# Chunk chain with its products grouped by kind and the next level's operand made early, and row transposes spread over the attention rounds

## The reference, cut to what matters

```python
zs = z[..., :SHIFT_COLS]                                   # 1792 columns
zs_mix = zs + w['mu_shift'] * (prev - zs)                  # prev: the row before
# RWKV-7 recurrence, a state of 64 x 64 per head, 8 heads
def step(s, inp):
    r_t, d_t, k_t, v_t, kk_t, a_t = inp
    sa = jnp.einsum('bhij,bhj->bhi', s, kk_t)
    s = (s * d_t[:, :, None, :] - sa[..., None] * (kk_t * a_t)[:, :, None, :]
         + v_t[..., None] * k_t[:, :, None, :])
    return s, jnp.einsum('bhij,bhj->bhi', s, r_t)
# forgetting attention of the prompt, 128 queries at a time
s = jnp.einsum('bqhd,bkhd->bhqk', q_i, k) * scale + F_i - Fk     # causal
p = jax.nn.softmax(s, axis=-1)
# attention of the samples over 4096 cached tokens: softmax(...) @ past_v
return y, k, v, logf, wkv_new, zs[:, -1]                   # also outputs
```

## Time and profile before

| what | us |
|---|---|
| median of 3 runs | 2940.16 (2926.0 to 2944.49) |
| the profiled execution: its own time | 2937.45 |
| its span on the core | 2935.7 |
| from the end of `z13` to the first scores of FOX (308.4 to 337.6) | 29.2 |
| FOX (337.6 to 600) | 262.4 |
| CHAIN (743 to 1160) | 417.0 |
| of which the four stretches of levels | 61.1, 64.3, 62.8, 63.0 |
| and the four stretches of two chunks | 31.9, 30.7, 30.3, 29.0 |
| QUERY's end and PEER (1510 to the end) | 1425.7 |

### The profile page before, as it was taken

One profiled execution on the slowest core, in us unless ns is written; L12 is line 12 of the kernel. 1 busy time (PEld: TensorE's weight loads), 2 busy tenths in 40 slices (PEclk: granted clock), 3 DMA queues, 4 the chain that ended last, 5 costly groups with the idle time before them and its releaser, 6 DMA issues.

```text
span 2935.7 us, 29533 instructions
## 1 busy us (share of the span) xinstructions
PE 2215.7 (75%) x9678; PEld 881.1 (30%) x9678; DVE 1666.6 (57%) x3582; ACT 240.9 (8%) x476; POOL 1353.8 (46%) x1559
## 2 busy tenths in 40 slices
PE   5999699942799898685892057777677777777998
PEld 3345355531454454342551011111111111111222
DVE  2588477547321221515279976676666667666812
ACT  1111211121010111100100000000000000000000
POOL 0233122100223332000058877777777777777755
PEclk7999789966878988897896589999999999999989
DMA  7377455435445545131079899999999999999988
GB/s 257 126 255 233 154 191 180 144 102 190 136 138 186 159 154 195 40 135 57 33 277 329 287 371 409 407 405 385 379 399 408 408 379 392 401 408 406 404 322 315
DMA packets 238555, 774.79 MB, mean 264 GB/s; under 512 B 32360, under 2 KB 34124, under 8 KB 237912
## 3 DMA queue, kind: packets, MB, share of 16 engines
q0 software_dynamic: 191008, 680.63, 62.7%
q1 hardware_dynamic: 47424, 92.54, 9.0%
HBM read 763.01 MB, written 10.04 MB: 263 GB/s over the span
## 4 chain that ended last, share of the span: by engine, by line
PE 39%; POOL 25%; DVE 14%; issue 12%; DMA 4%; POOLq 3%; ACT 1%; SPq 1%; PEldq 0%; DVEq 0%; ACTq 0%; PEld 0%
POOL arena L739 25%; PE bank L764 18%; DVE arena L2056 5%; PE bank L1186 5%; PE bank L907 3%; POOLq L717 2%; PE bank L903 2%; PE bank L1027 2%; DMA arena<-in_peer_v,arena 2%; PE bank L770 1%; SPq L563 1%; PE bank L1220 1%; PE bank L894 1%; PE bank L895 1%; PE bank L1084 1%
## 5 line engine op out<-in xcount | busy, mean ns | idle before, releaser
L1186 PE MATMUL bank<-arena 128*32 128x512 f32 x2048 | 889.6, 607 | 280.0 <-DMA arena<-in_peer_v,arena 275.8
L2056 DVE CUSTOM_DVE_ANT_0 arena<-arena 128x1024 f32<-128x1024 f32 x512 | 623.5, 1223 | 329.6 <-DMA arena<-in_peer_u,arena 328.0
L739 POOL DMA_INDIRECT arena<-in_peer_u,arena x520 | 566.2, 1089 | 501.8 <-DVE arena L1927 319.0
L764 PE MATMUL bank<-arena 128*128 128x8 f32 (+5 forms) x2088 | 589.8, 433 | 44.8 <-DVE arena L1772 23.9
L739 POOL DMA_INDIRECT arena<-in_peer_v,arena x520 | 509.8, 980 | 193.0 <-issue 141.6
L1186 PEld LDWEIGHTS bank<-arena 128*32 128x32 f32 x2048 | 180.2, 110 | 984.2 <-DMA arena<-in_peer_v,arena 654.3
L764 PEld LDWEIGHTS bank<-arena 128*128 128x128 f32 (+3 forms) x2088 | 309.4, 185 | 320.8 <-issue 282.9
L722 POOL DMA_DIRECT2D arena<-in_cache_v x256 | 137.7, 538 | 449.8 <-PE bank L1027 274.3
L722 POOL DMA_DIRECT2D arena<-in_cache_k x256 | 137.8, 538 | 414.1 <-issue 223.3
L770 PE MATMUL bank<-arena 128*128 128x128 f32 (+5 forms) x350 | 64.8, 323 | 244.2 <-DVE arena L1927 79.5
L1554 DVE TENSOR_TENSOR arena<-arena 128x512 f32<-128x512 f32 x256 | 175.4, 685 | 68.9 <-ACT arena L1242 51.0
(11 more groups left out here) (252 smaller groups left out, 1524.7 us busy)
## 6 DMA issues: line engine op xcount, KB each, us to landing
arena<-in_cache_k POOLq DMA_DIRECT2D x256, 256.0 KB, 3.5
arena<-in_cache_v POOLq DMA_DIRECT2D x256, 256.0 KB, 3.4
arena<-in_w_ada SPq DMA_DIRECT2D x12, 2048.0 KB, 10.5
arena<-in_w_in SPq DMA_DIRECT2D x10, 2048.0 KB, 10.3
arena<-in_peer_u,arena POOLq DMA_INDIRECT x520, 6.6
arena<-in_peer_v,arena POOLq DMA_INDIRECT x520, 6.6
arena<-in_peer_wq SPq DMA_DIRECT2D x4, 2048.0 KB, 7.9
arena<-scratch_gates SPq DMA_DIRECT2D x16, 260.0 KB, 2.7
```

Source lines behind the costliest of these rows:

```text
L739: nc.gpsimd.indirect_dma_start(gathered[:, j, :], None, tables[kind[0]][:, :], OFF(ap=index, axis=0)).then_inc(row_in[j], 16)
L764: ins = mm(out, a, b, start=i == 0, stop=i == len(pairs) - 1, **more)
L1186: ins = mm(acc[u][32 * j:32 * (j + 1), :], spread[:, token(x), :], gathered_row(("v", t, x))[:, 512 * u:512 * (u + 1)], start=x < 4, stop= ...
L2056: release(nc.vector.tensor_tensor_reduce(out=row, in0=row, in1=h2[:, t, :], scale=1.0, scalar=0.0, op0=MUL, op1=ADD, accum_out=act_of[t % ...
```

## The change

Three things are changed in PROJ and FOX. The eight row jobs (`shift0` to `shift3`, `krows0` to `krows3`) leave the end of PROJ; they are made in rounds 1, 5, 9, ..., 29 of FOX, their stores follow the gate stores on SP's queue, and the next writer of their buffer waits for the store's own semaphore. The exponential and logarithm of the forget logits are taken by ACT behind `z10`, and DVE's sum along the tokens behind its addition for block 11. The one addition of 7280 columns becomes 14 of 512 columns, each behind a share of the cached key pages, and one small one for the samples.

Two things are changed in CHAIN. DVE makes the next level's `xt` as soon as `iy` has been read, ahead of the two subtractions; PE waits for `inv` ahead of `iy` and for `inv_t` ahead of `inv`. In `r` and `oc` two matmuls with a buffer of zeros first open the whole sum (64 partitions, 256 columns each, one for each half of the partitions), then come the eight products over 64 partitions, then the eight over 128.

```diff
+ROWS_OUT = {4 * u + 1: f"shift{u}" for u in range(4)}
+ROWS_OUT.update({4 * t + 17: f"krows{t}" for t in range(NT)})
...
@@ sync @@
-            for u in range(4):
-                read(sp, f"shift{u}")
...
-                sp.wait_ge(stored, OUTPUTS[0])
-                sp.sem_inc(shift_stored, 1)
...
             for m in range(16):
                 read(sp, f"gc{m}")
                 load(scratch_g[:, m, 0:T], gate_rows[:, m % 2, :], gates_out[m % 2])
+                if m % 2 == 0 and m < 8:
+                    u = m // 2
+                    read(sp, f"shift{u}")
...
+                if m % 2 == 0 and m >= 8:
+                    t = m // 2 - 4
+                    read(sp, f"krows{t}")
+                    load(nk[:, t, :], buf("k_rows"), krows_out)
@@ tensor, FOX @@
+                if i in ROWS_OUT:
+                    job = ROWS_OUT[i]
+                    o = begin(job)
+                    if i < 16:
+                        for k in range(min(4, MS - (i - 1))):
+                            ins = turn(o[0:9, P * k:P * (k + 1)], z9[:, i - 1 + k, :])
+                    else:
+                        t = (i - 17) // 4
+                        for c in range(NC):
+                            ins = turn(o[:, P * c:P * (c + 1)], k_t[:, c, P * t:P * (t + 1)])
+                    end(ins, job)
@@ tensor, CHAIN @@
+                def open_sums(o):
+                    for a in (0, C):
+                        mm(o[a:a + C, 0:NC * C], ident[a:a + C, a:a + C], buf("zeros")[a:a + C, :], start=True, stop=False)
                 for lv in range(LEVELS):
                     pe.wait_ge(xt_ready, 2 * (gp * LEVELS + lv + 1))
+                    if lv:
+                        read(pe, f"inv{gp}_{lv - 1}")
                     small(f"iy{gp}_{lv}", xt, inv)
                     page_values(gp, 3 * lv, points)
                     read(pe, f"iy{gp}_{lv}")
+                    if lv:
+                        read(pe, f"invt{gp}_{lv - 1}")
...
                     o = begin(f"r{n}")
+                    open_sums(o)
                     for h, c, a in heads:
-                        mm(o[a:a + C, C * c:C * (c + 1)], rk[a:a + C, c, n, 0:C], state[a:a + C, c, :],
-                           start=True, stop=False)
-                        ins = mm(o[a:a + C, C * c:C * (c + 1)], g[:, e2, h, 0:C], uv[:, s, h, :], start=False, stop=True)
+                        mm(o[a:a + C, C * c:C * (c + 1)], rk[a:a + C, c, n, 0:C], state[a:a + C, c, :], start=False, stop=False)
+                    for h, c, a in heads:
+                        ins = mm(o[a:a + C, C * c:C * (c + 1)], g[:, e2, h, 0:C], uv[:, s, h, :], start=False, stop=c == NC - 1)
@@ scalar, PROJ @@
+                if m == 10:
+                    act.wait_ge(f_abs, 1)
+                    link(fn(f2[0:8, 0:TT], f2[0:8, 0:TT], ACT.Exp))
+                    link(fn(f2[0:8, 0:TT], f2[0:8, 0:TT], ACT.Ln, bias=1.0), signal=f_log, at=1)
@@ vector, PROJ @@
-            page_dots(96, 136)
...
-            link(tt(buf("mix"), buf("mix"), buf("prev"), ADD))
+            for m in range(MS):
+                page_dots(96 + 40 * m // MS, 96 + 40 * (m + 1) // MS)
+                read(dve, f"z{m}")
+                link(tt(mix[:, m, 0:T], mix[:, m, 0:T], prev[:, m, 0:T], ADD))
...
@@ vector, CHAIN @@
-                for lv in range(LEVELS):
-                    if lv:
-                        full(dve, f"iy{gp}_{lv - 1}")
+                def level(lv):
...
+                level(0)
+                for lv in range(LEVELS):
+                    if lv + 1 < LEVELS:
+                        full(dve, f"iy{gp}_{lv}")
+                        level(lv + 1)
```

More of the change, by code:

```diff
@@ L136 @@
     ("wring0", 4096, LOAD, QUERY), ("wring1", 4096, LOAD, QUERY),
-    ("mix", MS * TT, PROJ, MIX), ("prev", MS * TT, PROJ, PROJ), ("z9", MS * 9, PROJ, PROJ),
+    ("mix", MS * TT, PROJ, MIX), ("prev", MS * TT, PROJ, PROJ), ("z9", MS * 9, PROJ, FOX),
     ("shift_out", 512, PROJ, SAMPLE),
@@ L188, in psum_jobs @@
     fixed(7, "zs")
-    ring(*[f"shift{u}" for u in range(4)], *[f"krows{t}" for t in range(NT)], "logf")
+    ring("logf")
     fixed(7, "gs")
@@ L196, in psum_jobs @@
             ring(f"gc{i // 2}")
+        if i in ROWS_OUT:
+            ring(ROWS_OUT[i])
         if 2 <= i < NT * H + 2:
@@ L868, in _ @@
             read(pe, "zs")
-            for u in range(4):
-                o = begin(f"shift{u}")
-                for i in range(min(4, MS - 4 * u)):
-                    ins = turn(o[0:9, P * i:P * (i + 1)], z9[:, 4 * u + i, :])
-                end(ins, f"shift{u}")
-            for t in range(NT):
-                o = begin(f"krows{t}")
-                for c in range(NC):
-                    ins = turn(o[:, P * c:P * (c + 1)], k_t[:, c, P * t:P * (t + 1)])
-                end(ins, f"krows{t}")
             pe.wait_ge(logf_ready, 1)
@@ L1095, in _ @@
                     o = begin(f"oc{n}")
+                    open_sums(o)
                     for h, c, a in heads:
-                        mm(o[a:a + C, C * c:C * (c + 1)], state[a:a + C, c, :], rk[a:a + C, c, n, C:P],
-                           start=True, stop=False)
-                        ins = mm(o[a:a + C, C * c:C * (c + 1)], uv[:, s, h, :], g[:, e2, h, C:P], start=False, stop=True)
+                        mm(o[a:a + C, C * c:C * (c + 1)], state[a:a + C, c, :], rk[a:a + C, c, n, C:P], start=False, stop=False)
+                    for h, c, a in heads:
+                        ins = mm(o[a:a + C, C * c:C * (c + 1)], uv[:, s, h, :], g[:, e2, h, C:P], start=False, stop=c == NC - 1)
                     end(ins, f"oc{n}")
@@ L1287, in _ @@
                 take(f"z{m}", z9[:, m, 8:9], o[:, T - 1:T])
+                if m == 10:
+                    act.wait_ge(f_abs, 1)
+                    link(fn(f2[0:8, 0:TT], f2[0:8, 0:TT], ACT.Exp))
+                    link(fn(f2[0:8, 0:TT], f2[0:8, 0:TT], ACT.Ln, bias=1.0), signal=f_log, at=1)
             take("zs", z9[:, :, 0:8], bank("zs")[:, 0:MS * NS].rearrange("p (m b) -> p m b", m=MS))
-            for u in range(4):
-                n = min(4, MS - 4 * u) * P
-                if u:
-                    act.wait_ge(shift_stored, u)
-                take(f"shift{u}", buf("shift_out")[0:9, 0:n], bank(f"shift{u}")[0:9, 0:n])
-            for t in range(NT):
-                if t:
-                    act.wait_ge(krows_out, t)
-                take(f"krows{t}", buf("k_rows"), bank(f"krows{t}")[:, :])
-            act.wait_ge(f_abs, 1)
-            link(fn(f2[0:8, 0:TT], f2[0:8, 0:TT], ACT.Exp))
-            link(fn(f2[0:8, 0:TT], f2[0:8, 0:TT], ACT.Ln, bias=1.0), signal=f_log, at=1)
             take("logf", buf("logf_out"), bank("logf")[:, 0:NT * H])
@@ L1322, in _ @@
                     take(f"gc{m}", gate_rows[:, m % 2, :], bank(f"gc{m}")[:, :])
+                if i in ROWS_OUT and i < 16:
+                    u = i // 4
+                    n = min(4, MS - 4 * u) * P
+                    if u:
+                        act.wait_ge(shift_stored, 32 * u)
+                    take(f"shift{u}", buf("shift_out")[0:9, 0:n], bank(f"shift{u}")[0:9, 0:n])
+                if i in ROWS_OUT and i >= 16:
+                    t = (i - 17) // 4
+                    if t:
+                        act.wait_ge(krows_out, 16 * t)
+                    take(f"krows{t}", buf("k_rows"), bank(f"krows{t}")[:, :])
                 if i >= 3 and (i - 3) % H == H - 1:
@@ L1328, in _ @@
             act.wait_ge(gates_out[1], 8 * 16)
+            act.wait_ge(shift_stored, 4 * 32)
+            act.wait_ge(krows_out, NT * 16)
             act.wait_ge(proj_stored, 1)
@@ L1717, in _ @@
                 link(nc.vector.memset(removed[a:a + C, :, :, a // C, :], 0.0))
+            link(nc.vector.memset(buf("zeros"), 0.0))
             link(nc.vector.memset(buf("state"), 0.0), signal=state_ready, at=1)
```

31 lines of the change are left out of this document (17 added, 14 removed).

## The result

| | before | changed |
|---|---|---|
| median of 4 runs | 2937.51 (2926.0 to 2944.49) | 2901.78 (2892.78 to 2917.92) |
| profiled execution: its own time | 2937.45 | 2901.79 |
| its span | 2935.7 | 2900.1 |

The ratio of the times is 0.9872, with a 95% interval of 0.9838 to 0.9907. The gain is 36 us: inside the range, and smaller than the 54 of the forecast.

The account below looks back on a forecast made before the run. Bounds: a chain of waits before FOX, PE in FOX and CHAIN's chunks, POOL's page issuing in the levels. Terms -25.8 + 5 - 1 - 32 = -53.8 gave 2886.4, stated as 2885, range 2867 to 2903.

Parts of the forecast that it names:

- The stretch before FOX: End of PROJ: FOX starts at 311.8 instead of 337.64, -25.8 us, with bounds of -24.8 and -26.1.
- Forecast +4: FOX: +5 us for 30 added transposes (bounds 4 and 8.1), together with -1 for the clock.
- The -1 for a clock that rises sooner: FOX's first rounds: a shorter gap before them removes some low-clock time, -1 us, between 0 and -2.
- Forecast -32: CHAIN's chunks: shorter sums save 36.6 us, late pages take some back; bounds -24 to -37.
- The term that was mis-sized: CHAIN, `r` and `oc`: each sum takes 0.70 + 0.58 + 0.68 = 1.96 us instead of 4.54 and 3.96.
- a rival at 12%: CHAIN's chunks: the clock stays up without the alternation, perhaps 2 us a group more, 2877 in all; 12%.
- the 1.2 us a group of the forecast: CHAIN's chunks: time put down for pages that arrive late once the sums are shorter, 1.2 us a group.
- Halves of the array in one bank: CHAIN's sums: the halves do not overlap in a shared bank, a sum takes 2.98 us, 2898 in all; 10%.
- The early `xt`: CHAIN's levels: worth 0, as PE's 19.6 us wait becomes waiting for pages; rival of full -19.6, 2866, 4%.
- FOX's banks: FOX: row jobs put successive gate blocks in one bank, PE waits for ACT's gate copy, 2902 in all; 8%.
- the slow CHAIN: CHAIN: PE waits more and its clock falls; at 0.60 the kernel takes 2988, slower than before; 2%.
- What comes after CHAIN only starts earlier: Phases behind CHAIN, PEER included: they begin earlier and keep their length, 0 us.

Follow-up runs that it names:

- two later kernels: Kernel before with only its buffers moved: 3048.74, ratio 1.0019; kernel before with only the PROJ and FOX changes, buffers also moved: 3028.57, ratio 0.9939.
- a second queue: Changed kernel, with SP reading page numbers and issuing four of every eight value pages beside POOL: 2919.04 us, ratio 0.9532 to the kernel before.

## Why the prediction was right, and where it was not

**The stretch before FOX: right.** Forecast 311.8, measured 310.9, -26.7 for -25.8. I had let the last addition start when `zs` is read, and it starts when `z13` is read: that was the bound of -26.1. The functions behind `z10`, the stores behind the gates and the 13 additions cost nothing that shows.

**FOX: right within its scatter, its price somewhat too high.** Forecast +4, measured +5.6 in the two profiles, and 5.1 between the means of all executions (269.0 of eight with the jobs, 263.9 of five without), which scatter by 12. At a clock of 0.89 the transposes cost 3.3, less than the 4 that I had as the lower bound. That bound was half of a lone transpose's 0.27, which is a length from start to end; from start to start one in a row takes about 0.1 (thirty in 2.9 to 3.2). The -1 for a clock that rises sooner did not come: the first scores take 0.79 us for two instructions as they took 0.80 before. The changed kernel's FOX at 266.1 lies inside the "265 to 268", but its other executions show that this test could not tell anything.

**CHAIN: the mechanism right, the size too small.** Forecast -32, measured -41.4 in the profile and -36 over all executions. The four stretches of two chunks went from 121.9 to 86.4 us (21.6, 21.1, 22.4, 21.3), -35.5; the levels from 251.2 to 248.0; the rest lies between them. Three things made the profile's number larger than the forecast.
- The term that was mis-sized is the sum: it takes 1.66 us in `r` and 1.56 in `oc`, and not 1.96. Most of this is the opening, 0.48 and not 0.70. Its row was taken in FOX, two instructions from start to end, while the four of the opening, of 256 columns each, would be 0.90 one behind the other (3.60 / 8 / 2 each), 0.45 side by side. That is 0.30 us in eight sums and 0.40 in eight, 5.6.
- The clock in the chunks rose to 1.00 in all four groups, from 0.78 in the one of the earlier trace rows. This was a rival at 12%, and it took place together with the forecast. As I had said there, POOL caps what it is worth: 16 pages at 1.31 are 20.9 us, and the chunks stand at 21.1 to 22.4. So POOL took back more than the 1.2 us a group of the forecast. By the shorter sums alone (4.54 - 1.66 and 3.96 - 1.56, eight times each) the chunks would have lost 42.2 us and not 35.5, and PE is now idle for 2.7 to 3.8 us in each group's chunks.
- The old CHAIN took 417.9 in the profile that I worked from, and 407.0 and 411.8 in the two later kernels that have its instructions. This is scatter and no error of a term.

One reading in that part was wrong without harm to the sum: "about 0.26 us for every change of kind" is the whole sum divided by its changes, with the products' own time in it. Beyond the products a change cost about 0.17 us, by the `oc` that had the full clock ((3.96 - 1.18) / 16).

**Halves of the array in one bank: the rival refuted.** By it a sum would take 2.98 us; it takes 1.66, and the opening and the products over 64 partitions pass at the pace of `iy` (16 in 0.57, 32 in 1.15). The rule of the Trainium skill (TensorEngine Tiling (Array Packing), Restrictions and Gotchas), that different row tiles cannot access one PSUM bank at the same time, does not describe the time of these products.

**The early `xt`: right.** Worth 0 with one queue and 14.1 with two. The test named before the run, levels unchanged, one wait gone and the other grown, came out (61.4 to 62.7 a group; 19.6 to 6.2; 21.3 to 36.6).

**FOX's banks and the slow CHAIN: did not happen.** PE does not wait at the row jobs, and the clock in CHAIN rose from 0.87 to 0.94 while PE's busy time fell from 372 to 327.

**"What comes after CHAIN only starts earlier": the step that failed.** It costed PEER at 0, and in the first comparison PEER took 26.9 us more, 22.0 of them in its first full tile, at 378 GB/s instead of 404. Without this the profile would have shown -62.5, 9 more than the forecast; with it -35.6, 18 fewer. In the runs that followed neither the earlier start nor the addresses did it, since PEER takes 1565.6 and 1564.5 us there with and without the change, and the gain is 67 us. What set the bandwidth of that tile is open. The four runs of the changed kernel in the first comparison have their median at the profiled one, so it was no single bad execution. Whether PEER gets less bandwidth there when it begins at 1410 us, or the difference lies between the sets of runs, no run here can tell, since later runs fell on conditions where PEER takes about 100 us more throughout. That the time still fell inside the range, 1.2 us below its upper end, is luck: the range reached up for another reason, a longer sum in CHAIN, and CHAIN's 9 us beyond the forecast took up a third of the loss. For a kernel that spends half its time on gathers from memory, a spread of this phase, 1% of the whole, belongs into the range as a case of its own.

## What to carry to other kernels

Look for the engine that issues transfers as a bound of its own: here POOL was 35% busy in the changed kernel's CHAIN (133.63 of 376.54 us), waited for nobody in the levels, and set their pace by reading page numbers and issuing, 1.31 us a page. A wait shortened in such a stretch turns into another wait; a second queue was worth 80 us, more than the whole change.

Group small matmuls by the number of partitions they go over. Every change of kind cost about 0.17 us beyond the products themselves, and without the changes the clock was higher as well.

Before a difference of a few us in a stretch that TensorE bounds is explained, multiply its busy time by the granted clock, and run the same kernel twice.

## What the runs showed of the hardware that I had not expected

- The granted clock of FOX is 0.87 in some executions and 0.91 in others, for the same instructions and the same kernel, and moves 260 us by up to 12.
- The clock of the chunks went from 0.78 to 1.00 when 16 alternations of kind in a sum became two, while PE went from 99% busy to 85%. Which of the two did it was not separated; PE had been busy throughout when the old clock fell to 0.50 behind the alternating sums, and the levels with two queues, 98% busy and with no alternation but that with the pages, had 0.92.
- SP and POOL issuing from page numbers side by side moved 248 GB/s in the levels of the first group, where POOL alone moved 172.
- PEER took 1463 and 1490 us in the first comparison and 1565 to 1589 in the later ones, and the kernel before went from 2937.51 us to 3044.55 and more.
- Eight products over 64 partitions alternating with eight over 128 took 3.96 us at the full clock; grouped, the same sixteen take 1.18.
